# A layer with expert retrieval on one core: 49 gathered pairs moved behind, one dense tile chosen with the queries, half of the later one-hots on VectorE

## The chip, the cores and the metric

One core of one Trainium2 chip. The metric is the device time of one execution in microseconds; a lower one is better. A profiled execution lists its instructions from the first to the last (the span); its own time lies a little above that.

## The reference, cut to what matters

One layer (attention in two forms, then an expert retrieval, then an RMSNorm) is applied to a sample of 256 tokens and a prompt of 1024. The change touches only the expert retrieval of the prompt:

```python
def one_chunk(xc):                                   # 128 tokens
    qry = einsum('cd,dq->cq', xc, w_query)           # 8 heads, 2 halves of 128
    sc = einsum('chpd,hpnd->chpn', qry, sub_keys)    # 128 scores a half
    s_top, i_top = top_k(sc, 16)
    cand = s_top[half 0] + s_top[half 1]             # 16 x 16
    best_s, pos = top_k(cand, 16)
    idx = i_top[half 0] * 128 + i_top[half 1], at pos
    g = softmax(best_s)
    act = gelu(einsum('chkd,cd->chk', expert_u[idx], xc))
    return einsum('chk,chkd->cd', g * act, expert_v[idx])
```

There are 16384 experts; each token takes 128 slots (8 heads of 16), a row of u and one of v for each, 1024 floats wide.

## The kernel before, in words

The last phase, `phase_mixed`, computes this for the eight prompt tiles of 128 tokens in two ways. Five tiles are **gathered** (`GATHERED`): GpSimd fetches the 128 rows of a slot (u and v, 8 KB each, 1.05 MB in all) by an indirect DMA (L1894) into a ring of eight slots. VectorE takes the dot of the u half with h (L2155), ScalarE the gelu (L1984), VectorE multiplies it by the gate (L2147), ScalarE spreads it on small diagonals (L1991), and TensorE adds up the weighted v halves by 32 matmul records a pair of slots (L2289). A pair is a step; a tile has 65 steps with its last, five tiles have 325. GpSimd may fetch a pair when the pair four before it has been used by TensorE.

Three tiles are **dense** (`DENSE`: tiles 5, 6 and 7, 384 tokens together). All experts are computed for them: stage 1 (L2309) multiplies u, turned, by the 384 tokens, ScalarE takes the gelu (L2015), VectorE multiplies by a full matrix of gates (`mult`, L2180), stage 2 (L2325) multiplies by v, and VectorE adds the products up (L2190). This goes in 32 chunks of four key columns, each with 2 MB of u, 2 MB of v and 0.75 MB of gates loaded by SP's queue. The gates matrix is built before, in 96 **blocks** of four tokens (32 a tile): VectorE makes one-hot rows of the first index, times the gate (L2139), ScalarE one-hot rows of the second index by |iota - j| and relu(1 - x) (L1964, L1966), TensorE multiplies them (L2274), ScalarE copies the product out (L1973), and after every eight blocks it issues a store of 2 MB to `gates_d` (L1977) from one of two buffers. A block may begin when the block two before it has been multiplied. Ahead of each dense tile's blocks TensorE turns its indices and gates (`turn`, L2263) and ScalarE copies them (L1950).

Both ways need the choice of the experts. Queries (L2239) and scores (L2253) of all tiles are computed first, 32 queries of 16 matmul records, and the scores go to memory. SP loads them head by head into `SCL` buffers (L1775). A **pick** of a head is the two top-16 lists, the candidates and their top 16 (`choose`, L2049 to L2076); after four heads come the **decode** (L2083 to L2106) and the softmax of the gates.

One list sets the order of all this on every engine: `Turns.walk`. Each engine walks the same list and carries out its own part, in order. `advance(k)` puts k steps there, together with the picks of the gathered tiles that fall due by their step number (`octet`, L1544, L1545). The walk has three parts: the queries (L1574 to L1596), where steps begin with v = 13; the blocks (`turned` and the loops, L1614 to L1625); and the dense part (L1641 to L1655), where the steps left are spread evenly over the units of stage 1 and stage 2 by their cost (L1650):

```python
self.advance(before + round(rest * min(1.0, spent / whole)) - self.e, False)
```

## Time and profile before

| | us |
|---|---|
| median of 3 runs | 4753.62 (4751.6 to 4756.91) |
| the profiled execution, its own time | 4752.96 |
| its span | 4751.2 |
| TensorE busy | 4023.7 (85%) |
| VectorE busy | 2817.4 (59%) |
| ScalarE busy | 1179.1 (25%) |
| GpSimd busy | 1241.0 (26%) |
| read and written in memory | 1366 MB, 288 GB/s over the span |

The shares are means over phases with different limits; the phase that changes begins near 2095 us. A busy TensorE counts matmuls whose ends are modelled. In the rows PE is TensorE, PEld its loading of weights, DVE VectorE, ACT ScalarE, POOL GpSimd, SP the sync engine's queue; L12 is line 12 of the kernel, and an arrow `<-` stands before what is read or waited for. A DMA share is the mean busy share of the core's 16 DMA engines.

### The profile page before, as it was taken

How to read it: one execution, taken by the hardware profiler on the slowest of the kernel's cores; microseconds unless marked ns; L12 is line 12 of the kernel's file. 1: busy time of each engine (PE TensorE's matmuls, PEld its weight loads, DVE VectorE, ACT ScalarE, POOL GpSimd, SP SyncE). 2: the span in 40 equal slices, each digit the busy share in tenths (PEclk: the TensorE clock that was granted, in tenths of full speed). 3: DMA queues.
4: the chain of work that ended last, by engine and by line, in shares of the span. 5: the costliest groups of instructions: out<-in, count | busy, mean ns of one | idle time of the engine just before them, and what ended most of it. 6: DMA issues, size and time to landing. Idle time of an engine off the chain costs nothing.

```text
span 4751.2 us, 61482 instructions
## 1 busy us (share of the span) xinstructions
PE 4023.7 (85%) x22629; PEld 2075.0 (44%) x22629; DVE 2817.4 (59%) x7082; ACT 1179.1 (25%) x3076; POOL 1241.0 (26%) x1018
## 2 busy tenths in 40 slices
PE   7786699996999989979864444589999999999998
PEld 3444444443777754434321222334444444444443
DVE  1323865775888867634668888735454554545434
ACT  0221111221555531121213544711111111111111
POOL 0201322222344223301332233322222222222221
PEclk9888799998999999989875767799999999999999
DMA  6143498986444377646898988999998999889996
GB/s 239 66 173 120 165 360 301 372 334 234 158 165 185 136 305 297 263 182 254 340 356 320 364 336 348 367 341 344 364 362 323 363 359 362 336 335 346 355 359 249
DMA packets 351291, 1370.43 MB, mean 288 GB/s; under 512 B 26896, under 2 KB 112528, under 8 KB 231568
## 3 DMA queue, kind: packets, MB, share of 16 engines
q0 software_dynamic: 129024, 939.58, 50.8%
q1 hardware_dynamic: 161840, 389.17, 22.4%
q10 hardware_dynamic: 60128, 37.75, 2.5%
q8 instruction: 180, 2.95, 0.2%
q14 instruction: 119, 0.97, 0.1%
HBM read 1277.22 MB, written 89.18 MB: 288 GB/s over the span
## 4 chain that ended last, share of the span: by engine, by line
PE 34%; DVE 11%; DMA 7%; issue 3%; ACT 2%; POOL 0%; SPq 0%; DVEq 0%; ACTq 0%; POOLq 0%
PE prompt_exp_wk L2309 13%; PE prompt_exp_wk L2325 11%; PE prompt_exp_acc L2289 6%; DVE prompt_exp_junk L2155 4%; DMA prompt_exp_ring<-in_experts_dram,prompt_exp_idx 3%; PE prompt_exp_wk L2239 3%; DMA gates_dram<-prompt_exp_area 2%; ACT prompt_exp_diag L1991 1%; DVE prompt_exp_topi L2052 1%; DVE prompt_exp_hit L2101 1%; DVE prompt_exp_hT L2139 1%; DVE prompt_exp_top L2049 1%; DMA scores_dram<-prompt_exp_area 1%; DVE prompt_exp_rest L2057 0%; POOL prompt_exp_ring L1894 0%
## 5 line engine op out<-in xcount | busy, mean ns | idle before, releaser
L1894 POOL DMA_INDIRECT prompt_exp_ring<-in_experts_dram,prompt_exp_idx x640 | 686.8, 1073 | 1977.6 <-PE prompt_exp_acc L2289 1758.0
L2155 DVE CUSTOM_DVE_ANT_0 prompt_exp_junk<-prompt_exp_ring,prompt_exp_h 128x1024 bf16<-128x1024 f32 x640 | 761.2, 1221 | 112.2 <-DMA prompt_exp_ring<-in_experts_dram,prompt_exp_idx 112.1
L2309 PE MATMUL prompt_exp_wk<-prompt_exp_hT,prompt_exp_area 128*128 128x384 f32 x2048 | 692.1, 492 | 16.2 <-DMA prompt_exp_area<-in_u_turned_dram 16.2
L2325 PE MATMUL prompt_exp_wk<-prompt_exp_area 128*128 128x512 f32 x1536 | 698.2, 603 | 0.0
L2289 PE MATMUL prompt_exp_acc<-prompt_exp_ring,prompt_exp_diag 32*32 32x512 f32 x10240 | 414.4, 677 | 225.2 <-ACT prompt_exp_diag L1991 224.0
L2190 DVE TENSOR_TENSOR prompt_exp_area<-prompt_exp_area,prompt_exp_wk 128x512 f32<-128x512 f32 x186 | 127.6, 686 | 776.9 <-PE prompt_exp_wk L2325 755.6
L537 PE MATMUL prompt_proj_acc<-normed_w,normed_hT 128*128 128x512 f32 x1280 | 553.8, 595 | 14.4 <-PEq L91 14.4
L2309 PEld LDWEIGHTS prompt_exp_wk<-prompt_exp_hT,prompt_exp_area 128*128 128x128 f32 x2048 | 385.0, 191 | 343.5 <-issue 88.4
L152 POOL DMA_INDIRECT sample_hid_ring<-in_experts_dram,sample_hid_idx x256 | 275.1, 1075 | 898.3 <-DVE sample_hid_acc L182 849.3
L2325 PEld LDWEIGHTS prompt_exp_wk<-prompt_exp_area 128*128 128x128 f32 x1536 | 283.8, 191 | 409.5 <-issue 378.3
L1984 ACT ACTIVATE prompt_exp_ge<-prompt_exp_dot 128x2 f32<-128x2 f32 x320 | 64.8, 203 | 1301.9 <-DVE prompt_exp_dot L2155 1301.4
L537 PEld LDWEIGHTS prompt_proj_acc<-normed_w,normed_hT 128*128 128x128 f32 x1280 | 243.6, 191 | 318.5 <-issue 318.3
L165 DVE CUSTOM_DVE_ANT_0 sample_hid_junk<-sample_hid_ring,sample_hid_h 128x1024 bf16<-128x1024 f32 x256 | 353.9, 1382 | 37.5 <-DMA sample_hid_ring<-in_experts_dram,sample_hid_idx 27.5
L182 DVE SCALAR_TENSOR_TENSOR sample_hid_acc<-sample_hid_ring,sample_hid_w,sample_hid_acc 128x1024 f32<-128x1024 f32 x254 | 330.5, 1301 | 7.4
L2274 PE MATMUL prompt_exp_wk<-prompt_exp_area,prompt_exp_hT 128*128 128x128 f32 x768 | 148.9, 362 | 186.1 <-DVE prompt_exp_hT L2139 137.1
L2289 PEld LDWEIGHTS prompt_exp_acc<-prompt_exp_ring,prompt_exp_diag 32*32 32x32 f32 x10240 | 81.3, 108 | 442.9 <-ACT prompt_exp_diag L1991 350.0
L2274 PEld LDWEIGHTS prompt_exp_wk<-prompt_exp_area,prompt_exp_hT 128*128 128x128 f32 x768 | 132.9, 265 | 249.1 <-DVE prompt_exp_hT L2139 185.3
L2015 ACT ACTIVATE prompt_exp_area<-prompt_exp_wk 128x384 f32<-128x384 f32 x128 | 62.7, 490 | 436.2 <-PE prompt_exp_wk L2309 436.0
L1991 ACT ACTIVATE prompt_exp_diag<-prompt_exp_fold,prompt_exp_wgt 128x32 f32<-128x32 f32 x640 | 165.9, 306 | 16.3 <-DVE prompt_exp_wgt L2147 16.3
L537 PE MATMUL sample_proj_acc<-sample_proj_w,sample_proj_hT 128*128 128x512 f32 x320 | 139.5, 598 | 9.4 <-PEq L271 9.4
L998 PE MATMUL prompt_att_Op<-prompt_att_vB,prompt_att_pT_b 128*128 128x128 f32 x1024 | 125.9, 276 | 10.4 <-ACT prompt_att_pT_a L712 10.4
L1964 ACT ACTIVATE prompt_exp_area<-prompt_exp_iota,prompt_exp_ijgT 128x128 f32<-128x128 f32 x384 | 121.9, 389 | 21.2 <-issue 16.6
(350 smaller groups left out, 5001.5 us busy)
## 6 DMA issues: line engine op xcount, KB each, us to landing
prompt_exp_area<-in_u_turned_dram SPq DMA_DIRECT2D x128, 512.0 KB
prompt_exp_area<-in_experts_dram SPq DMA_DIRECT2D x64, 1024.0 KB
gates_dram<-prompt_exp_area ACTq DMA_DIRECT2D x12, 2048.0 KB, 25.0
prompt_exp_area<-gates_dram SPq DMA_DIRECT2D x32, 768.0 KB, 10.7
sample_proj_w<-in_w_all_dram SPq DMA_DIRECT2D x10, 2048.0 KB, 20.0
normed_w<-in_w_all_dram SPq DMA_DIRECT2D x10, 2048.0 KB, 18.6
proj_dram<-prompt_proj_stage SPq DMA_DIRECT2D x80, 256.0 KB
prompt_exp_ring<-in_experts_dram,prompt_exp_idx POOLq DMA_INDIRECT x640
```

What stands on the lines that cost most here:

```text
L152: self.nc.gpsimd.indirect_dma_start(out=self.ring[:, s % self.RING, :], out_offset=None, in_=self.experts, in_offset=bass.IndirectOffsetOn ...
L165: self.nc.vector.tensor_tensor_reduce(out=self.junk[:], in0=self.ring[:, s % self.RING, 0:D], in1=self.h[:], scale=1.0, scalar=0.0, op0=AL ...
L182: nc.vector.scalar_tensor_tensor(self.acc[:], v, w, self.acc[:], ALU.mult, ALU.add).then_inc(self.added, 1)
L537: last = nc.tensor.matmul(acc[:, u % 4, :], hT[:, k, t * P:(t + 1) * P], w[:, c % NL, k, :], start=(k == 0), stop=(k == KD - 1))
L1894: nc.gpsimd.indirect_dma_start(out=ring[:, s % RING, :], out_offset=None, in_=experts, in_offset=bass.IndirectOffsetOnAxis(ap=idx[:, n % 2 ...
L1991: last = nc.scalar.activation(diag[:, (g - 1) % 2, c, :], fold[:], ACT.Copy, scale=wgt[:, s:s + 1])
L2155: nc.vector.tensor_tensor_reduce(out=junk[:, s % 2, :], in0=ring[:, s % RING, 0:D], in1=h2[:, n % 2, :], scale=1.0, scalar=0.0, op0=ALU.mu ...
L2239: last = nc.tensor.matmul(wk[:, v % 2, :], wq[:, h // 2 % 2, k, at:at + P], (hT1 if grp else hT0)[:, k, :], start=(k == 0), stop=(k == KD ...
L2274: last = nc.tensor.matmul(wk[:, 2 + i % 2, c * KEYS:(c + 1) * KEYS], onehot_a[:, i % 2 * BLOCK + c, :], onehot_b[:, i % 2, c, :], start=Tr ...
L2289: last = nc.tensor.matmul(acc[at:at + Q, part, :], diag[k, (g - 1) % 2, c, :], ring[k, s % RING, D + half * 512:D + half * 512 + 512], sta ...
L2309: last = nc.tensor.matmul(wk[:, j % 2, 0:TURNED], ut[:, j % 3, k, :], hT_dense[:, k, :], start=(k == 0), stop=(k == KD - 1))
L2325: last = nc.tensor.matmul(wk[:, 2 + o % 2, :], act_e[:, c % 2, j, t * P:(t + 1) * P], vt[:, half, j, :], start=(j == 0), stop=(j == JB - 1))
```

## The change

It changes the order and three resources, not what is computed.

- In the query part two steps a query become one and two by turns, and the second dense tile (6) is picked there, beside tile 5. Tile 7's picks stand in the first tile's blocks.
- The first tile's blocks have one step for every two of them, the second tile's one for every four, the third's three for every eight.
- Since two dense tiles are chosen before the first turn, tile 6 has its own buffers: `mid`, `mid_ij`, `mid_gd` in a free piece of `area`, and a third kind in `topi` and `pos`. `SCL` goes from 4 to 3.
- From block 32 on, the second one-hot rows of every odd block are made by VectorE, in one instruction of 128x512 (`is_equal` of iota and the index, both broadcast), and not by ScalarE's five.

The diff, with some context and unchanged parts left out:

```diff
--- before.py
+++ after.py
@@ -1592,8 +1592,10 @@
                 on("gates", GATHERED[0], slice(ends[h], h + 1))
             if 0 <= h < HEADS and at == 2:
                 self.pick_dense(first, h)
+            if h >= 0 and at == 3 and h < HEADS:
+                self.pick_dense(first + 1, h)
             if v >= 13:
-                self.advance(2)
+                self.advance(1 + v % 2)
         done = 0
 
         def blocks(k):
@@ -1611,18 +1613,19 @@
             on("turn", d)
             self.advance(1)
 
-        for d in range(2):
+        turned(0)
+        for k in range(HEADS):
+            self.pick_dense(first + 2, k)
+            for _ in range(2):
+                blocks(2)
+                self.advance(1)
+        for d in (1, 2):
             turned(d)
-            for k in range(HEADS):
-                self.pick_dense(first + d + 1, k)
+            for k in range(BLOCKS // 4):
                 blocks(2)
-                self.advance(2 if k % 2 else 1)
+                self.advance(k % 2 if d == 1 else 1)
                 blocks(2)
-                self.advance(2)
-        turned(2)
-        for k in range(BLOCKS // 2):
-            blocks(2)
-            self.advance(1)
+                self.advance(1 - k % 2)
         on("spread_b", done - 1)
         on("built")
         assert done == len(DENSE) * BLOCKS
@@ -1667,7 +1670,7 @@
 
     with ExitStack() as ctx:
         m = Mem(nc, ctx, [], tag)
-        RING, SCL = 8, 4
+        RING, SCL = 8, 3
         BACK = RING // PAIR
         NQ = P // Q
         NG, ND = len(GATHERED), len(DENSE)
@@ -1677,25 +1680,28 @@
         junk = m.sb("junk", [P, 2, D], mybir.dt.bfloat16)
         ysq, yo = m.sb("ysq", [P, 2, D]), m.sb("yo", [P, D])
         hT0, area = m.sb("hT0", [P, KD, 512]), m.sb("area", [P, 16384])
-        top, topi = m.sb("top", [P, 2, TOPK]), m.sb("topi", [P, 2, 2, 4, TOPK], U32)
+        top, topi = m.sb("top", [P, 2, TOPK]), m.sb("topi", [P, 3, 2, 4, TOPK], U32)
         topb, table = m.sb("topb", [P, 2, 4, TOPK], BF16), m.sb("table", [P, 2, TOPK], BF16)
         rest = m.sb("rest", [P, 2, KEYS])
         cand, crest = rest[:, 0, 0:CANDS], rest[:, 1, 0:CANDS]
         best, soft, ssum = m.sb("best", [P, 3, HEADS, TOPK]), m.sb("soft", [P, 3, HEADS, TOPK]), m.sb("ssum", [P, HEADS])
-        pos, posf = m.sb("pos", [P, 2, 2, 4, TOPK], U32), m.sb("posf", [P, 2, 4, TOPK])
+        pos, posf = m.sb("pos", [P, 3, 2, 4, TOPK], U32), m.sb("posf", [P, 2, 4, TOPK])
         part, ab = m.sb("part", [P, 2, 4, TOPK]), m.sb("ab", [P, 2, 4, TOPK], BF16)
         hit = m.sb("hit", [P, 4, TOPK, TOPK], BF16)
         idx, g2 = m.sb("idx", [P, 2, SLOTS], I32), m.sb("g2", [P, 2, SLOTS])
         dot, ge, wgt = (m.sb(n, [P, SLOTS]) for n in ("dot", "ge", "wgt"))
         diag = m.sb("diag", [P, 2, PAIR, Q])
         scl = m.sb("scl", [P, SCL, 2 * KEYS])
-        ij, gd, ijgT = m.sb("ij", [P, 2, SLOTS]), m.sb("gd", [P, SLOTS]), m.sb("ijgT", [P, 2, 3, P])
+        ij_sb, gd_sb, ijgT = m.sb("ij", [P, 2, SLOTS]), m.sb("gd", [P, SLOTS]), m.sb("ijgT", [P, 2, 3, P])
...
+        mid = area[:, 15360:15616].rearrange("p (a h k) -> p a h k", a=2, h=HEADS)
+        mid_ij, mid_gd = area[:, 15616:15872].rearrange("p (a s) -> p a s", a=2), area[:, 15872:16000]
+        ij, gd = ij_sb[:], gd_sb[:]
         scs = area[:, 14336:15360].rearrange("p (x c) -> p x c", x=2)
...
@@ -1749,6 +1755,27 @@
...
+        def vector_b(i):
+            return i >= BLOCKS and i % 2 == 1
+
+        def scalar_bs(count):
+            return sum(not vector_b(i) for i in range(count))
+
+        def kind_of(tile):
+            return 0 if tile in GATHERED else 1 + (tile - DENSE[0]) % 2
+
+        def best_of(tile):
+            return mid[:, 0] if kind_of(tile) == 2 else best[:, place(tile)]
+
+        def soft_of(tile):
+            return mid[:, 1] if kind_of(tile) == 2 else soft[:, place(tile)]
+
+        def ij_of(d):
+            return mid_ij if d % 2 else ij
+
+        def gd_of(d):
+            return mid_gd if d % 2 else gd
 
         def normed(k):
             return hs_[:, k, :] if k else h2[:, 0, :]
@@ -1939,7 +1966,7 @@
                     nonlocal softened
                     softened += 1
                     act.wait_ge(best_ready, softened)
-                    part = soft[:, place(tile), hs, :]
+                    part = soft_of(tile)[:, hs, :]
                     nc.scalar.activation(part, part, ACT.Exp).then_inc(exp_ready, 1)
 
                 def turn(d):
@@ -1957,8 +1984,10 @@
...
+                    if vector_b(i):
+                        return
                     if i:
-                        act.wait_ge(b_ready, i)
+                        act.wait_ge(b_ready, scalar_bs(i))
...
@@ -2060,7 +2089,7 @@
 
                 def choose(tile, h, part):
                     nonlocal picked
-                    o, c, kind = place(tile), h % 4, int(tile in DENSE)
+                    c, kind = h % 4, kind_of(tile)
                     if part == 0:
                         dve.wait_ge(scl_ld[picked % SCL], 16 * (picked // SCL + 1))
                         top16([(top[:, p, :], topi[:, kind, p, c, :], scl[:, picked % SCL, p * KEYS:(p + 1) * KEYS], rest[:, p, :])
@@ -2075,10 +2104,10 @@
...
@@ -2091,9 +2120,9 @@
                     link(nc.vector.scalar_tensor_tensor(ab[:, 1, c, :], row, 9.0, part[:, 1, c, :], ALU.is_lt, ALU.mult))
                     cols = slice(hs.start * TOPK, hs.stop * TOPK)
                     if tile in DENSE:
-                        if tile > DENSE[0] and hs.start == 0:
-                            dve.wait_ge(ij_turned, tile - DENSE[0])
-                        to = ij[:, :, cols]
+                        if tile == DENSE[2] and hs.start == 0:
+                            dve.wait_ge(ij_turned, 1)
+                        to = ij_of(tile - DENSE[0])[:, :, cols]
                     else:
                         to = part[:, :, c, :].rearrange("p a h k -> p a (h k)")
                     found = hit[:, 0:n, :, :]
@@ -2107,20 +2136,18 @@
                         dve.sem_inc(heads_chosen[tile], n)
 
                 def soften(tile, hs):
-                    o = place(tile)
-                    nc.vector.tensor_tensor(soft[:, o, hs, :], best[:, o, hs, :],
-                                            best[:, o, hs, 0:1].to_broadcast([P, hs.stop - hs.start, TOPK]),
+                    nc.vector.tensor_tensor(soft_of(tile)[:, hs, :], best_of(tile)[:, hs, :],
+                                            best_of(tile)[:, hs, 0:1].to_broadcast([P, hs.stop - hs.start, TOPK]),
                                             ALU.subtract).then_inc(best_ready, 1)
 
                 def gates(tile, hs):
                     nonlocal gated
                     gated += 1
-                    o = place(tile)
-                    to = gd[:] if tile in DENSE else g2[:, tile % 2, :]
+                    to = gd_of(tile - DENSE[0]) if tile in DENSE else g2[:, tile % 2, :]
                     dve.wait_ge(exp_ready, gated)
-                    link(nc.vector.reduce_sum(ssum[:, hs], soft[:, o, hs, :], AXX))
+                    link(nc.vector.reduce_sum(ssum[:, hs], soft_of(tile)[:, hs, :], AXX))
                     link(nc.vector.reciprocal(ssum[:, hs], ssum[:, hs]))
-                    link(nc.vector.tensor_tensor(to.rearrange("p (h c) -> p h c", c=TOPK)[:, hs, :], soft[:, o, hs, :],
+                    link(nc.vector.tensor_tensor(to.rearrange("p (h c) -> p h c", c=TOPK)[:, hs, :], soft_of(tile)[:, hs, :],
                                                  ssum[:, hs].unsqueeze(2).to_broadcast([P, hs.stop - hs.start, TOPK]), ALU.mult))
 
                 def turn(d):
@@ -2134,6 +2161,10 @@
                         dve.wait_ge(q_full, 32)
                     if i >= 2:
                         dve.wait_ge(gp_full, i - 1)
+                    if vector_b(i):
+                        wide = [P, BLOCK, KEYS]
+                        nc.vector.tensor_tensor(onehot_b[:, i % 2, :, :], iota[:].unsqueeze(1).to_broadcast(wide),
+                                                ijgT[:, d % 2, 1, BLOCK * k:BLOCK * k + BLOCK].unsqueeze(2).to_broadcast(wide), ALU.is_equal)
                     for c in range(BLOCK):
                         t = BLOCK * k + c
                         last = nc.vector.tensor_scalar(onehot_a[:, i % 2 * BLOCK + c, :], iota[:], ijgT[:, d % 2, 0, t:t + 1],
@@ -2259,13 +2290,13 @@
                     pe.wait_ge(q_ready, 32)
                     if d:
                         pe.wait_ge(ij_spread, d)
-                    for a, x in enumerate((ij[:, 0, :], ij[:, 1, :], gd[:])):
+                    for a, x in enumerate((ij_of(d)[:, 0, :], ij_of(d)[:, 1, :], gd_of(d))):
                         last = nc.tensor.transpose(wk[:, 0, a * P:(a + 1) * P], x, ident[:])
                     last.then_inc(ij_turned, 1)
 
                 def block_(i):
                     pe.wait_ge(a_ready, i + 1)
-                    pe.wait_ge(b_ready, i + 1)
+                    pe.wait_ge(b_ready, scalar_bs(i + 1))
                     if i < 2:
                         pe.wait_ge(s_ready, 32)
                     else:
```

## Rows read from the trace of the kernel before

**Rows 1.** The page: busy tenths of TensorE and the DMA engines in 40 slices.

```profile
PE   7786699996999989979864444589999999999998
...
DMA  6143498986444377646898988999998999889996
```

**Rows 2.** Stretches, busy us (x instructions) of PE, PEld, DVE, ACT, POOL; clock; DMA share; GB/s.

```profile
2210.00:2450.00 240.00, 201.59 (x1616) 86.18 (x1584) 152.63 (x482) 47.48 (x151) 76.98 (x73) 0.90 0.90 348
2450.00:2551.00 101.00, 34.07 (x499) 8.32 (x499) 80.12 (x281) 16.31 (x54) 30.75 (x31) 0.52 0.89 358
2551.00:2762.00 211.00, 100.31 (x1203) 55.93 (x1203) 182.40 (x646) 102.94 (x291) 63.61 (x60) 0.67 0.87 331
2762.00:2971.00 209.00, 95.88 (x1221) 55.08 (x1219) 181.08 (x628) 98.64 (x290) 62.96 (x59) 0.70 0.91 350
2971.00:3093.00 122.00, 69.42 (x816) 43.63 (x816) 91.70 (x285) 88.71 (x249) 42.41 (x36) 0.79 0.98 367
3093.00:3143.00 50.00, 33.75 (x186) 17.67 (x183) 16.64 (x50) 8.26 (x21) 5.79 (x5) 0.83 0.82 297
3143.00:4733.00 1590.00, 1548.99 (x9547) 697.31 (x9546) 755.25 (x1746) 199.65 (x715) 396.83 (x372) 0.99 0.92 347
```

**Rows 3.** ScalarE's copies of the turned tiles, L1950.

```profile
L1950 ACT COPY prompt_exp_ijgT<-prompt_exp_wk x3: 478/478/478, 2550.8 to 2970.9; 128x384 f32<-128x384 f32 x3
```

**Rows 4.** Stage-1 matmuls of the dense part, L2309.

```profile
L2309 PE MATMUL prompt_exp_wk<-prompt_exp_hT,prompt_exp_area x2048: 486/486/1009, 3093.1 to 4699.5; 128*128 128x384 f32 x187
```

**Rows 5.** Order in time on ScalarE, 2999 to 3013 us.

```profile
2999.74 7.96 ACTq L1977 DMA_DIRECT2D gates_dram<-prompt_exp_area  x1
...
3012.34 0.58 ACT L1973 COPY prompt_exp_area<-prompt_exp_wk 128x512 f32<-128x512 f32 x1 [2.60 <-DMA gates_dram<-prompt_exp_area]
```

**Rows 6.** Gates stores, L1977: issue on ScalarE's queue, time to landing.

```profile
L1977 ACTq DMA_DIRECT2D gates_dram<-prompt_exp_area x12: 366/370/8425, 2606.9 to 3091.7; - x12
...
DMA to landing us min/median/max: 19.0/25.0/34.2
```

**Rows 7.** TensorE's groups in 3143 to 4720: busy us, mean ns, idle before.

```profile
L2289 PE MATMUL prompt_exp_acc<-prompt_exp_ring,prompt_exp_diag 32*32 32x512 f32 x5984 | 216.6, 607 | 36.4 <-ACT prompt_exp_diag L1991 35.2 <-DVE prompt_exp_ysq L2166 1.3
```

**Rows 8.** Order in time on VectorE, 2975 to 3012 us.

```profile
2977.13 0.48 DVE L2049 MAX8 prompt_exp_top<-prompt_exp_scl 128x8 f32<-128x128 f32 x2
...
2981.98 2.14 DVE L2139 TENSOR_SCALAR prompt_exp_hT<-prompt_exp_iota,prompt_exp_ijgT 128x128 f32<-128x128 f32 x8
2984.03 0.15 DVE L2147 TENSOR_TENSOR prompt_exp_wgt<-prompt_exp_ge,prompt_exp_g 128x2 f32<-128x2 f32 x1
...
2986.39 2.14 DVE L2139 TENSOR_SCALAR prompt_exp_hT<-prompt_exp_iota,prompt_exp_ijgT 128x128 f32<-128x128 f32 x8
...
3002.45 0.22 DVE L2083 CAST prompt_exp_topb<-prompt_exp_topi 128x128 bf16<-128x128 uint32 x1
...
3009.30 1.22 DVE L2104 TENSOR_REDUCE prompt_exp_part<-prompt_exp_hit 128x64 f32<-128x1024 bf16 x1
```

**Rows 9.** VectorE's groups in 2551 to 2971: busy us, mean ns, idle before.

```profile
L2155 DVE CUSTOM_DVE_ANT_0 prompt_exp_junk<-prompt_exp_ring,prompt_exp_h 128x1024 bf16<-128x1024 f32 x117 | 139.7, 1220 | 23.9 <-DMA prompt_exp_ring<-in_experts_dram,prompt_exp_idx 23.9
...
L2101 DVE TENSOR_TENSOR prompt_exp_hit<-prompt_exp_ab,prompt_exp_table 128x1024 bf16<-128x1024 bf16 x12 | 14.7, 1225 | 0.4
...
L2147 DVE TENSOR_TENSOR prompt_exp_wgt<-prompt_exp_ge,prompt_exp_g 128x2 f32<-128x2 f32 x59 | 9.2, 156 | 17.7 <-ACT prompt_exp_ge L1984 16.0 <-issue 1.0
```

**Rows 10.** DMA in 3143 to 4720: in all, and the gathers' queue.

```profile
DMA packets 111819, 551.25 MB, mean 350 GB/s; under 512 B 9744, under 2 KB 11664, under 8 KB 64016
...
q0 software_dynamic: 53665, 390.76, 64.0%
```

**Rows 11.** DMA in 2675 to 2725: busy tenths of 40 slices, and in all.

```profile
DMA  9999999999999999999999999999999999999999
...
DMA packets 7063, 20.08 MB, mean 402 GB/s; under 512 B 351, under 2 KB 4821, under 8 KB 5015
```

**Rows 12.** Waits in 2225 to 2450: us in total, times, longest.

```profile
DVE prompt_exp_junk L2155 <- DMA prompt_exp_ring<-in_experts_dram,prompt_exp_idx: 66.8, 38, 3.1
```

More of the change, by code:

```diff
@@ L2077, in choose @@
                                                  top[:, 1, 0:1].to_broadcast([P, TOPK - HALF_ROWS]), ALU.add))
-                    top16([(best[:, o, h, :], pos[:, kind, 0, c, :], cand, crest)])
+                    top16([(best_of(tile)[:, h, :], pos[:, kind, 0, c, :], cand, crest)])
                 def decode(tile, hs):
-                    n, kind = hs.stop - hs.start, int(tile in DENSE)
+                    n, kind = hs.stop - hs.start, kind_of(tile)
                     c, square = slice(hs.start % 4, hs.start % 4 + n), [P, n, TOPK, TOPK]
```

## The prediction

> **What bounds the kernel now.** I read the page first: over the last third TensorE stands at nine tenths, and the DMA engines stand at eight or nine tenths in nearly all of the second half [rows 1]. So there are two candidates, TensorE and the DMA engines, and an average cannot choose between them. The table by stretches does [rows 2]. I cut it at the three turns (where ScalarE copies a turned tile: 2550.8, 2762 and 2970.9 us, the first and the last of three in [rows 3]) and at the first stage-1 matmul (3093.1 us [rows 4]). Five stretches matter:
>
> - 2210 to 2450, queries with gathered steps beside them: TensorE 201.6 of 240 us, DMA share 0.90.
> - 2450 to 2551, the end of the query part: VectorE 80 of 101 us, TensorE 34.
> - 2551 to 2762 and 2762 to 2971, the blocks of the first two dense tiles: VectorE 182.4 of 211 and 181.1 of 209 us. VectorE sets these.
> - 2971 to 3093, the blocks of the third tile: VectorE 92, ScalarE 89 of 122 us, but DMA share 0.98. Here the DMA engines set the pace: the issue of a gates store took 7.96 us [rows 5] where the median is 0.37 [rows 6], and a copy behind it waited 2.60 us for a store to land [rows 5].
> - 3093 to the end, the dense part: in 3143 to 4733 TensorE is busy 1549 of 1590 us at a granted clock of 0.99, so at the 2.4 GHz level. Its step matmuls waited for ScalarE's diagonals 35.2 us in all [rows 7]. TensorE sets this part. But the DMA engines are at 0.92 beside it, 347 GB/s. They are the next bound, and a close one.
>
> **The change by its parts.** Counting the walk (the list of calls is the same for all engines): the steps issued at the three turns and at the end of the blocks were 53, 83, 113, 130 and become 40, 58, 68, 81, of 325. So 49 steps, 98 row gathers of 1.05 MB, 102.8 MB, go from the part ahead into the dense part.
>
> *Prices.* From the order in time on VectorE [rows 8]: a step is 2.36 us where it waits for nothing (2984.03 to 2986.39), a pick 4.85 (2977.13 to 2981.98), a decode of four heads 8 (from 3002.45; its last big reduction starts at 3009.30). In the first two tiles' blocks the dots waited 23.9 us and the weights 17.7 over 59 steps, 0.7 a step [rows 9]; so a step removed gives between 2.4 and 3.1, and I take 3.0, since these waits are the steps' own. A step on TensorE: 216.6 us busy for 187 steps (5984 records at 32 a step) = 1.16 us [rows 7]. A one-hot by one VectorE instruction of 128x512, both inputs broadcast: not in the trace. The nearest is the comparison of 128x1024 bf16 elements with broadcast inputs at 1225 ns [rows 9]: half of it, 0.61, for 512 elements. The ends are 0.5 (a float row may start cheaper) and 1.23 (a float element may cost two of bf16); I use 0.7, near the half. There are 32 of them, 22 us, between 16 and 39.
>
> *Query part, to the first turn* (before 2551). 13 steps leave; tile 6's eight picks and two decodes come in and tile 1's four picks go: on VectorE -39 + 19 + 16 = -4 us. Up to the last query VectorE has room (152.6 of 240 us [rows 2]), so there TensorE's side counts: 9 steps x 1.16 = -10. Behind the last query, where VectorE sets the pace, 13 steps instead of 17, five picks instead of seven, one decode more: -12 - 10 + 8 = -14. Together -24; the ends are 0 (the picks moved ahead delay the dots, and the queries with them) and -35.
>
> *First tile's blocks.* 12 steps fewer (30 to 18), one pick more (13 for 12): -36 + 5 = -31; 211 becomes 180. Ends -20 and -40.
>
> *Second tile's blocks.* 30 steps become 10, 11 picks one, three decodes none, 16 one-hots come: 209 - 60 - 10 x 4.85 - 24 + 11 = 87 us on VectorE. ScalarE's 98.6 us [rows 2] are for 32 blocks and 30 steps; with half of its one-hots and 20 steps gone it has some 55. What is late next is the gates store: four of 2 MB in this stretch, two buffers, so a stretch of eight blocks cannot be shorter than one store's landing, 25 us median, 19 to 34 [rows 6]. Four of them are 76 to 136. I take 95, near the VectorE sum and the median: -114, ends -75 and -124.
>
> *Third tile's blocks.* 17 steps become 13. The stretch is DMA-limited, and 8 gathers at 2.7 us of all 16 engines (0.640 x 1577 us for 390.76 MB [rows 10]) are 22 us; the store's latency stays: -17, ends 0 and -30.
>
> *Queues moved past.* With three score buffers for four, SP issues each score load one pick nearer to its use, and in order: it waits there for a buffer, with the loads of h and x behind it. Tile 6's eight loads now stand between the query part's. A pick that comes before its load holds every dot behind it on VectorE. The largest wait of a dot for a row was 3.1 us [rows 12]; I take +5 for the whole, from 0 to +15. POOL's order of gathers is the same, and a tile's decodes stay at the same step numbers, so it waits for no list longer than before. The third kind of buffers (topi, pos, mid) adds no instruction, only room; tile 7's decode still waits for the first turn, long past.
>
> Ahead of the dense part: -24 - 31 - 114 - 17 + 5 = **-181 us**; the blocks end near 2912.
>
> *Dense part.* Before it takes 3093 to 4751, 1658 us. For TensorE 49 steps at 1.16 add 57. VectorE takes 49 steps, six picks and two decodes more (45 picks stood ahead before, 39 do now): 118 + 29 + 16 = 163 us on 755 of 1590 [rows 2], hidden beside TensorE and the transfers. For the DMA engines, 566 MB (551 in 3143 to 4720 [rows 10] and 297 GB/s in the 50 us before [rows 2]) become 671 MB with 102.8 for the gathers and some 2 for scores and one more tile's h, x and output. At what rate? The engines' own figure is 347 at a share of 0.92 [rows 2], 377 at a full one. But the rate goes up where more is queued: 402 GB/s over 2675 to 2725, with small gates stores among the gathers, where the share was full [rows 11]. When the DMA engines are the bound, gathers and weights are queued always. I take 386, between 377 and 402 and nearer to the row of the same mix: 671 / 386 = 1738. To that come the tail without transfers, 4720 to 4751, 31 us; the thin start, 50 x (1 - 297/386) = 12; and some 10 for the closing of tiles. Sum 1791: **+133**, ends +57 (TensorE) and +209 (370 GB/s).
>
> The sum: 4752.96 (the profiled execution; its span of 4751.2 and 1.8 around it) - 181 + 133 = **4705**. The median of the runs, 4753.62, is 0.7 above the profiled one; nothing is corrected for it.
>
> **The rivals.**
>
> *TensorE stays the bound of the dense part*: then +57, 4753 - 181 + 57 = 4629. For it: TensorE waits for so little now, and rates above 400 exist [rows 11]. Against: 671 MB in 1640 + 57 us is 395 GB/s as a mean over the whole part, its thin start and every closing of a tile included. 0.14.
>
> *The DMA engines saturate at what they show per full share*: slower than before. The break-even rate follows from 1658 + 181 - 53 = 1786 us for 671 MB: 376 GB/s. Its place is the ring of eight rows: where steps come as densely as they will, in the queries, dots waited 66.8 us for rows in 225 us [rows 12]; TensorE was busy only 201.6 of 240 us there, and its granted clock was 0.90, between the levels of 1.2 and 2.4 GHz, so a part of that time ran at the lower [rows 2]. At 370 GB/s the dense part is 671 / 370 + 53 = 1867, +209, and the time 4781. For: 377 is what the dense rows give at full share, and 358 GB/s, share 0.89, is the rate of 2450 to 2551 [rows 2]. 0.25.
>
> *The rate does not rise at all with what is queued*: the 350 GB/s of the dense part [rows 10] is then a ceiling, 671 / 350 + 53 = 1970, +312, 4884. Against it stand 20 MB at 402 [rows 11]; these could be the exception. 0.03. Beside it stands a rule of the Trainium skill, "DMA: Bandwidth & Descriptors", section "Where 436 GB/s comes from": for transfers between HBM and SBUF the HBM side binds, at about 358 GB/s. By that figure the dense part would be an estimated 671 / 358 + 53 = 1927 us, and the kernel 4841. By that rule the trace agrees in the mean of the dense part and disagrees in the 50 us at 402.
>
> *The blocks do not get shorter as they should*: the gates stores and the picks moved ahead hold them, and only -110 of the -181 comes. Then 4753 - 110 + 133 = 4776, or about no change with a better dense rate. For: landings of 34.2 us exist [rows 6]. Against: gathers, which such a store shares the engines with, become a third as many there. 0.10.
>
> **How the numbers follow.** The forecast has 0.48, from 396 to 378 GB/s 4661 to 4742. A measurement here can tell about 0.2%, 9.5 us. Faster: 0.44 of the forecast, 0.14 of the first rival, 0.02 of the last: 0.60. Within 0.2%: 0.04 of the forecast, 0.06 of the second, 0.03 of the last: 0.13. Slower: 0.19, 0.03 and 0.05: 0.27. The range takes in the first rival's 4629 and the second's to some 366 GB/s, and with that the last rival: 4625 to 4800. What is left out is the ceiling at 350 and the tails.
>
> **What would show it.** Turns nearer to each other: first at about 2527, then +180, +95, and the first stage-1 matmul near 2912. VectorE's new group, 32 instructions near 0.7 us; ScalarE's Abs down from 384 to 256. In the dense part: DMA share 0.97 or more at 380 to 392 GB/s, VectorE waiting for rows, TensorE below 97% busy and a part of its time waiting for diagonals. I am wrong if the dense rate is under 376 (slower) or TensorE is as busy as before (much faster), or if the blocks end after 2950.

## The result and the profile after

The changed kernel takes 4601.75 us (median of 4 runs, 4596.18 to 4608.61), the kernel before 4752.61 beside it: a ratio of 0.9684, interval 0.9667 to 0.9701. It is 151 us faster, where 48 us had been forecast, and outside the range.

The kernel after was cut into stretches at its own three turns (2497.6, 2664.0 and 2759.7 us), its last query (2407.6) and its first stage-1 matmul (2855.8). The columns are those of [rows 2]: bounds, length, busy us (x instructions) of PE, PEld, DVE, ACT and POOL, granted clock, DMA share, GB/s.

```profile
2210.00:2407.60 197.60, 178.19 (x1264) 80.19 (x1263) 150.65 (x543) 41.94 (x123) 55.74 (x52) 0.94 0.84 319
2407.60:2497.60 90.00, 30.28 (x453) 8.85 (x451) 72.84 (x243) 15.69 (x47) 24.87 (x25) 0.56 0.81 315
2497.60:2664.00 166.40, 83.84 (x835) 56.25 (x835) 158.40 (x619) 91.41 (x253) 37.73 (x38) 0.66 0.76 279
2664.00:2759.70 95.70, 52.00 (x563) 37.59 (x563) 73.00 (x225) 59.16 (x148) 16.26 (x17) 0.84 0.83 297
2759.70:2855.80 96.10, 56.86 (x672) 40.39 (x673) 79.09 (x236) 55.25 (x153) 28.42 (x28) 0.84 0.99 365
2855.80:4599.50 1743.70, 1653.68 (x11362) 724.90 (x11361) 953.70 (x2251) 257.10 (x904) 528.09 (x475) 0.98 0.97 387
```

The same cuts in the kernel before, which the text reads below. [Rows 2] had its first two cuts at round times, so the queries' end (2442.4) differs a little:

```profile
2210.00:2442.40 232.40, 196.91 (x1535) 83.43 (x1504) 145.80 (x450) 45.31 (x145) 75.05 (x70) 0.90 0.90 351
2442.40:2550.80 108.40, 38.76 (x581) 11.07 (x579) 86.78 (x310) 18.29 (x59) 32.49 (x33) 0.56 0.89 353
3093.10:4751.20 1658.10, 1587.37 (x9780) 715.70 (x9776) 782.72 (x1808) 216.50 (x749) 402.63 (x376) 0.98 0.91 343
```

Part by part, in us:

| part | before | after | difference | forecast |
|---|---|---|---|---|
| queries and their end, to the first turn | 340.8 | 287.6 | -53.2 | -24 and +5 |
| first tile's blocks | 211.6 | 166.4 | -45.2 | -31 |
| second tile's blocks | 208.5 | 95.7 | -112.8 | -114 |
| third tile's blocks | 122.2 | 96.1 | -26.1 | -17 |
| ahead of the dense part | 883.1 | 645.8 | -237.3 | -181 |
| dense part | 1658.1 | 1743.7 | +85.6 | +133 |
| sum | | | -151.7 | -48 |

Two terms are off: what the steps were worth ahead of the dense part, and what they cost in it. (One of the 49 steps is the closing of a tile, which gathers nothing. So 48 pairs moved, 96 gathers and 100.7 MB, where the title and the prediction have 49, 98 and 102.8.) The new VectorE instruction is not one of them. Its group in the kernel after:

```profile
L2166 DVE TENSOR_TENSOR prompt_exp_area<-prompt_exp_iota,prompt_exp_ijgT x32: 676/688/699, 2666.6 to 2852.3; 128x512 f32<-128x512 f32 x32
```

The prediction assumed 0.7 us for it, and it takes 0.688. Now the dense part after. First the DMA engines in 2906 to 4568 (in all, and the gathers' queue), as in [rows 10]:

```profile
DMA packets 126802, 653.49 MB, mean 393 GB/s; under 512 B 11408, under 2 KB 14224, under 8 KB 66774
...
q0 software_dynamic: 67392, 490.76, 72.9%
```

then TensorE's steps in it, as in [rows 7] (busy us, mean ns, idle before):

```profile
L2320 PE MATMUL prompt_exp_acc<-prompt_exp_ring,prompt_exp_diag 32*32 32x512 f32 x7520 | 270.9, 604 | 44.4 <-ACT prompt_exp_diag L2020 43.4 <-DVE prompt_exp_ysq L2197 0.9
```

The rate rose from 350 to 393 GB/s, as the forecast had said it would under a longer queue. But TensorE's waits for diagonals rose only from 35.2 to 43.4 us, and TensorE is still busy 1653.7 of 1743.7 us. Both bounds are close here, and a profile with both near full does not say which of them ends last. That took runs.

### The profile page after: what moved, and what is told of

The parts are those of the page before. It is cut to its first block, busy times and chain, and to the rows that moved or that the text cites. A ratio compares the mean times of both kernels' runs of the same rounds, so it can differ in the third digit from the quotient of the medians.

```text
span 4599.5 us, 61350 instructions
## 1 busy us (share of the span) xinstructions
PE 3988.8 (87%) x22629; PEld 2057.9 (45%) x22629; DVE 2836.5 (62%) x7114; ACT 1128.4 (25%) x2916; POOL 1254.2 (27%) x1018
## 4 chain that ended last, share of the span: by engine, by line
PE 34%; DVE 10%; DMA 6%; issue 3%; ACT 2%; POOL 0%; SPq 0%; DVEq 0%; ACTq 0%; another core or an unknown queue 0%
PE prompt_exp_wk L2340 13%; PE prompt_exp_wk L2356 11%; PE prompt_exp_acc L2320 6%; DVE prompt_exp_junk L2186 4%; PE prompt_exp_wk L2270 4%; DMA prompt_exp_ring<-in_experts_dram,prompt_exp_idx 3%; DMA gates_dram<-prompt_exp_area 2%; DVE prompt_exp_hT L2170 1%; DVE prompt_exp_hit L2130 1%; DVE prompt_exp_topi L2081 1%; ACT prompt_exp_diag L2020 1%; PE prompt_exp_wk L2305 1%; DVE prompt_exp_top L2078 0%; DMA scores_dram<-prompt_exp_area 0%; PE prompt_exp_wk L2284 0%
## 5 line engine op out<-in xcount | busy, mean ns | idle before, releaser
L1921 POOL DMA_INDIRECT prompt_exp_ring<-in_experts_dram,prompt_exp_idx x640 | 698.6, 1092 | 1815.9 <-PE prompt_exp_acc L2320 1603.4
L2340 PE MATMUL prompt_exp_wk<-prompt_exp_hT,prompt_exp_area 128*128 128x384 f32 x2048 | 697.5, 495 | 23.7 <-DMA prompt_exp_area<-in_u_turned_dram 23.7
L2320 PE MATMUL prompt_exp_acc<-prompt_exp_ring,prompt_exp_diag 32*32 32x512 f32 x10240 | 392.9, 643 | 173.5 <-ACT prompt_exp_diag L2020 170.3
L2305 PE MATMUL prompt_exp_wk<-prompt_exp_area,prompt_exp_hT 128*128 128x128 f32 x768 | 132.7, 342 | 112.9 <-DVE prompt_exp_hT L2170 76.4
L2305 PEld LDWEIGHTS prompt_exp_wk<-prompt_exp_area,prompt_exp_hT 128*128 128x128 f32 x768 | 122.3, 250 | 157.8 <-DVE prompt_exp_hT L2170 102.3
L174 DVE TENSOR_TENSOR sample_hid_w<-sample_hid_ge,sample_hid_g 128x1 f32<-128x1 f32 (+1 forms) x208 | 59.1, 284 | 115.0 <-ACT sample_hid_ge L203 114.8
```

Source lines behind the costliest of these rows:

```text
L1921: nc.gpsimd.indirect_dma_start(out=ring[:, s % RING, :], out_offset=None, in_=experts, in_offset=bass.IndirectOffsetOnAxis(ap=idx[:, n % 2 ...
L2305: last = nc.tensor.matmul(wk[:, 2 + i % 2, c * KEYS:(c + 1) * KEYS], onehot_a[:, i % 2 * BLOCK + c, :], onehot_b[:, i % 2, c, :], start=Tr ...
L2320: last = nc.tensor.matmul(acc[at:at + Q, part, :], diag[k, (g - 1) % 2, c, :], ring[k, s % RING, D + half * 512:D + half * 512 + 512], sta ...
L2340: last = nc.tensor.matmul(wk[:, j % 2, 0:TURNED], ut[:, j % 3, k, :], hT_dense[:, k, :], start=(k == 0), stop=(k == KD - 1))
```

## The experiments

**Which part of the change gives the gain.** The change has three parts: 49 steps moved (S), tile 6 chosen with the queries (T), VectorE's one-hot rows (V). Four kernels took them apart.

The changed kernel without V:

```diff
         def vector_b(i):
-            return i >= BLOCKS and i % 2 == 1
+            return False
```

> The changed kernel with all second one-hot rows made by ScalarE again (VectorE's 32 instructions of 0.69 us gone, ScalarE's five back). Theory G (the gates stores and the DMA engines set the second and third tile's blocks, 96 us each): both stretches stay within 5 us, time 4602 to 4612. Theory E (the engines' own work sets them): ScalarE goes from 59 to about 88 us and from 55 to 84 of 96 us in them and waits more for TensorE between, so each gets 8 to 20 us longer, time 4618 to 4642.

4602.93 us, ratio 0.9684 (0.9668 to 0.9700), the same as with V. The second and third tile's blocks of this kernel:

```profile
2657.30:2757.00 99.70, 66.80 (x563) 48.01 (x563) 64.35 (x209) 86.58 (x229) 17.31 (x17) 0.72 0.81 284
2757.00:2857.20 100.20, 65.74 (x673) 44.27 (x673) 70.73 (x221) 82.38 (x234) 31.12 (x28) 0.75 0.99 359
```

ScalarE is at 87 and 82 of 100 us and not at 59 and 55 of 96. The stretches get 4 us longer each. In the whole time that does not show: the first turn of this profile comes 6.6 us earlier (2491.0 for 2497.6), in a part that V does not touch. Theory G's numbers came, both stretches within 5 us and the time in its range. So ScalarE's own work does not set these stretches; what holds them near 96 to 100 is not isolated here.

The kernel before with S alone:

```diff
-                self.advance(2)
+                self.advance(1 + v % 2)
...
-        for d in range(2):
+        for d in range(3):
             turned(d)
             for k in range(HEADS):
-                self.pick_dense(first + d + 1, k)
+                if d < 2:
+                    self.pick_dense(first + d + 1, k)
                 blocks(2)
-                self.advance(2 if k % 2 else 1)
+                self.advance(k % 2 if d == 1 else 1)
                 blocks(2)
-                self.advance(2)
+                self.advance(1 if d == 0 else 1 - k % 2)
-        turned(2)
-        for k in range(BLOCKS // 2):
-            blocks(2)
-            self.advance(1)
```

> The kernel before with only the steps moved: 40, 58, 68, 81 at the turns and the end of the blocks, tile 6 still picked in the first tile's blocks, ScalarE making all second rows, four score buffers. Theory of the prediction's sums (queries set by TensorE, a step 1.16 us there and 3.0 where VectorE sets the pace): queries -22, blocks -36, -60, -17, dense part +86: 4753 - 49 = about 4704. Theory R (in the queries the steps waited for their rows, so each step there is worth 3.5 to 5 us): queries -50, the rest the same: about 4675.

4622.40 us, ratio 0.9727 (0.9711 to 0.9744): 131 of the 151 us, and more than either theory gave. Its stretches up to the third turn:

```profile
2210.00:2388.30 178.30, 168.62 (x1209) 76.18 (x1208) 119.79 (x399) 39.26 (x116) 54.40 (x50) 0.97 0.89 344
2388.30:2468.40 80.10, 30.68 (x453) 9.85 (x451) 56.63 (x175) 15.80 (x46) 26.21 (x25) 0.57 0.89 358
2468.40:2635.60 167.20, 82.62 (x836) 56.57 (x835) 158.22 (x619) 91.34 (x253) 37.25 (x38) 0.68 0.76 278
2635.60:2770.40 134.80, 69.74 (x563) 50.51 (x563) 114.21 (x453) 87.50 (x228) 15.44 (x17) 0.69 0.63 219
```

The queries lost 54.1 us for 9 steps and their end 28.3 us for 4 steps and four picks, which fall due later with the steps. The 54.1 is a little too large. All these stretches are cut at 2210 us, but the query part does not begin at the same time in every profile. Taken from the first step's matmuls on TensorE (2209.7 us before, 2205.4 here) to the last query, the stretch went from 232.7 to 182.9 us. That is 49.8 us for 9 steps, 5.5 us for one, at much the same rate of the DMA engines (350 and 339 GB/s). The two row gathers of a step are 5.4 us of all 16 DMA engines, the price in the prediction; TensorE's 1.16 us is a fifth of the 5.5. The end lost about what the prediction's prices give, 4 x 3.0 + 4 x 4.85 = 31.

The blocks lost 44.4, 73.7 and 23.2 us, where both theories had 36, 60 and 17, and the queries with their end 82.4, where they had 22 and 50. The dense part of this kernel is 1744.3 us, as in the changed one and as both theories had it.

The kernel before with T alone (the step counts of before, ScalarE's rows):

```diff
+            if h >= 0 and at == 3 and h < HEADS:
+                self.pick_dense(first + 1, h)
...
-        for d in range(2):
+        turned(0)
+        for k in range(HEADS):
+            self.pick_dense(first + 2, k)
+            blocks(2)
+            self.advance(2 if k % 2 else 1)
+            blocks(2)
+            self.advance(2)
+        for d in (1, 2):
             turned(d)
             for k in range(HEADS):
-                self.pick_dense(first + d + 1, k)
                 blocks(2)
-                self.advance(2 if k % 2 else 1)
+                self.advance(1 if d == 2 or k % 2 == 0 else 2)
                 blocks(2)
-                self.advance(2)
+                self.advance(2 if d == 1 else 1)
```

> The kernel before with only tile 6 picked in the queries and tile 7 in the first tile's blocks (with its buffers, three score buffers), steps 53, 83, 113, 130 as before, no VectorE rows. By the prediction's sums VectorE has room of 87 us in the first 240 us of the queries, but 47 to 65 us of picks and decodes come in: the second tile's blocks lose 40 us of picks and 16 of decodes if nothing else sets them, the queries gain 0 to 30: time 4725 to 4750. Theory R (rows set the queries): what comes in is hidden in waits, and the second tile's blocks, with 30 steps and stores, become DMA-limited at about 170: 4715 to 4735. If the picks hold the dots back: 4753 or more.

4744.59 us, ratio 0.9981 (0.9971 to 0.9992), a gain of some 9 us and in the range of the first theory. Its second tile's blocks:

```profile
2775.40:2955.00 179.60, 95.76 (x1219) 52.64 (x1219) 131.55 (x384) 97.90 (x290) 64.78 (x59) 0.74 1.00 393
```

VectorE has 49 us less to do in them, but the stretch becomes 28.9 us shorter and no more: the DMA share is 1.00. In this stretch Theory R had the mechanism, with 170 us for 179.6. The picks that came into the queries and their end cost 14.4 us there. So T pays more where the steps are gone: beside S the second tile's blocks go from 134.8 (S alone) to 99.7 (S and T), and the time from 4622.4 to 4602.9.

The kernel before with V alone (the edits of the diff to `vector_b`, `scalar_bs` and `build_a`, without the others):

```diff
+                    if vector_b(i):
+                        wide = [P, BLOCK, KEYS]
+                        nc.vector.tensor_tensor(onehot_b[:, i % 2, :, :], iota[:].unsqueeze(1).to_broadcast(wide), ...)
```

> The kernel before with only VectorE making the second rows of every odd block from block 32. VectorE sets the second tile's blocks (181 of 209 us), so +11 us there; the third tile's are DMA-limited (share 0.98), 0. Time 4760 to 4768. If ScalarE's five instructions were on the chain there (a rival), the third stretch gets 10 us or more shorter and the time is 4745 to 4755.

4756.51 us, ratio 1.0006 (0.9996 to 1.0016): no difference that can be measured, and a time between the two expected ranges. In the profile the second tile's blocks took 214.0 us for 208.5 and the third's 120.9 for 122.2. That is the first theory's order with half of its cost. The profiled execution took 4771.04 us; most of what it lies above the median came in its queries, 11.9 us longer than before, which V does not touch.

**What sets the queries.** The kernel before with half of each query's matmuls; it leaves out half of the sum over d in the queries, and so picks other experts:

```diff
-                    for k in range(KD):
+                    for k in range(KD // 2):
...
-                                                start=(k == 0), stop=(k == KD - 1))
+                                                start=(k == 0), stop=(k == KD // 2 - 1))
```

> The kernel before with four of the eight matmuls of every query: it leaves out half of the sum over d, TensorE does some 110 us less in the queries, the transfers stay; the picks find other experts, so other rows are gathered, as many. Theory of the prediction (TensorE sets the queries up to the last one, 232 us from 2210): that stretch gets 50 to 60 us shorter for its 18 queries beside steps. Theory R (the steps wait for their rows there, at a DMA share of 0.90): from query 13 on it gets less than 25 us shorter; the time falls by what the first 13 queries give, 15 to 45 us, and little more.

4724.47 us, ratio 0.9934 (0.9917 to 0.9951). The queries with steps beside them, from the first step's matmuls to the last query, first before and then in this kernel:

```profile
2209.70:2442.40 232.70, 197.21 (x1536) 83.66 (x1536) 146.06 (x453) 45.31 (x145) 75.05 (x70) 0.90 0.90 350
2186.20:2420.20 234.00, 144.69 (x1392) 56.99 (x1393) 147.80 (x468) 45.69 (x147) 74.58 (x70) 0.77 0.87 342
```

TensorE is busy 53 us less here, and the stretch is no shorter. The 22 us by which the last query comes earlier were all gained ahead of the first step, where only queries run. That is Theory R. (One pick waited 17.1 us for its scores here and 4.8 before; with those 12 us taken off, the stretch would still be 222.) Nine steps fewer took 50 us off the same stretch. So it was not TensorE that set it, though it was busy for 85% of it; the steps' way through gather, dot, gelu, diagonal did. How much of the 5.5 us a step is transfer and how much the way back to a free ring slot, no run here separates.

**What sets the dense part.** Two kernels take a load away from one side each. The changed kernel with half of each u from the fourth on, so that stage 1 uses stale halves:

```diff
+                    ks = KD if j < 3 else KD // 2
-                    sp.dma_start(ut[:, j % 3, :, :], u_turned[j]...)
+                    sp.dma_start(ut[:, j % 3, 0:ks, :], u_turned[j]...[:, 0:ks, :])
```

> The changed kernel with only half of each turned u loaded from the fourth on: it leaves out 33 MB of 671 in the dense part and computes stage 1 with stale halves. Theory P: the dense part stays within 15 us of 1744 (the shorter loads may shorten its first stall by a few). Theory D: 33 MB at 393 GB/s are 83 us, dense part 1660 to 1680, time 4520 to 4535.

The changed kernel with four of the eight matmuls of each stage-1 product:

```diff
-                    for k in range(KD):
+                    for k in range(KD // 2):
...
-                                                start=(k == 0), stop=(k == KD - 1))
+                                                start=(k == 0), stop=(k == KD // 2 - 1))
```

> The changed kernel with only four of the eight matmuls of each stage-1 product: it leaves out half of the sum over d, TensorE does some 338 us less, and all transfers stay. The dense part then shows what the DMA engines can do. By the prediction's term they carry 671 MB at 386 GB/s, 1791 us: the dense part would stay at 1740 or more. If they can do 402 to 415 GB/s, and TensorE set the dense part: 671/402 to 671/415 + 50, 1665 to 1720, time 4520 to 4578. A time under 4500 would say that 420 GB/s is no bound.

Without 33 MB the time is 4589.97 us, some 12 less, not the 83 of Theory D. With TensorE relieved it is 4543.40, in the range given for a dense part that TensorE set. The dense part of each, first that of the kernel with half of u, then that of the one with half of stage 1:

```profile
2857.40:4590.90 1733.50, 1651.59 (x11362) 724.41 (x11360) 950.02 (x2249) 256.36 (x904) 530.89 (x474) 0.98 0.95 370
```

```profile
2855.50:4542.20 1686.70, 1385.48 (x10338) 550.36 (x10336) 955.34 (x2249) 249.84 (x904) 534.82 (x474) 0.94 0.99 399
```

So TensorE sets the dense part at 244 steps, and the DMA engines stand at most 57 us behind: they carry it in 1686.7 us, 399 GB/s with the start and the tail in it, at a share of 0.99. The prediction had 1791 for the same. TensorE is not alone, though: 268 us of its work gone gave only these 57.

**Where the DMA engines take over.** Fewer steps ahead, so more in the dense part. One step a query, 68 ahead:

```diff
-                self.advance(1 + v % 2)
+                self.advance(1)
```

> The changed kernel with one step a query, so 27, 45, 55, 68 steps at the turns and the end of the blocks, 13 fewer ahead. Theory P (TensorE still sets the dense part, a step costs there the 1.75 us that 49 steps cost in it): dense part +23; the queries, now at 0.84 DMA share and 178 of 198 us of TensorE, give 13 to 25 back: time 4600, between 4595 and 4612. Theory D (the DMA engines, share 0.97 in the dense part, set it already): 13 steps are 26 gathers at 2.6 us, dense part +68, time 4640 or more.

and with it one step for four blocks in the first tile's blocks, 60 ahead:

```diff
             for _ in range(2):
                 blocks(2)
-                self.advance(1)
+                self.advance(_)
```

> As the run with 68 ahead, and one step for four blocks in the first tile's blocks, so 27, 37, 47, 60. VectorE sets that stretch: 8 steps off it at 2.7 to 4 us give 22 to 32. Theory P: dense part +14 beyond the run with 68, so that time -8 to -18. Theory D: dense part +42 beyond it, so that time +10 to +20.

68 ahead: 4589.04 us (4585.98 to 4590.15), ratio 0.9656 (0.9638 to 0.9675). That is below the 4595 to 4612 of Theory P: the queries and their end became 40.2 us shorter, where 13 to 25 were expected. The first tile's blocks also became 20.6 shorter and the other two 18.1 longer, since picks fall due by the number of steps, and three of them and a decode left the first. 60 ahead: 4625.81, ratio 0.9736 (0.9717 to 0.9755), 37 us more than with 68, where even Theory D had 10 to 20. Its 8 steps gave 15.8 us in the first tile's blocks, not 22 to 32, and cost 62.2 in the dense part, not 42.

The dense part of each, first with 68 ahead, then with 60:

```profile
2813.10:4586.70 1773.60, 1669.33 (x11778) 726.53 (x11777) 995.67 (x2343) 267.09 (x944) 550.22 (x500) 0.98 0.98 395
```

```profile
2786.10:4621.90 1835.80, 1698.34 (x12018) 734.51 (x12016) 1019.09 (x2408) 275.99 (x970) 578.81 (x515) 0.97 0.97 390
```

| steps in the dense part | its time | for each step more | VectorE's dots waited for gathered rows, 2900 to 4560 |
|---|---|---|---|
| 195 | 1658.1 | | |
| 244 | 1743.7 | 1.75 | 116.8 |
| 257 | 1773.6 | 2.3 | 217.8 |
| 265 | 1835.8 | 7.8 | 245.6 |

Behind the first 100 us and up to the last 29, the same two:

```profile
2913.10:4557.70 1644.60, 1573.33 (x11106) 683.69 (x11105) 939.16 (x2229) 244.24 (x879) 525.99 (x477) 0.99 1.00 402
2886.10:4592.90 1706.80, 1612.53 (x11453) 696.43 (x11451) 970.25 (x2306) 250.61 (x907) 559.20 (x496) 0.98 1.00 400
```

At 257 steps the DMA engines have just become full (share 1.00, 402 GB/s), and the price of a step is still near Theory P's. Beyond, it jumps. The last 8 steps are seven pairs and the closing of a tile: 14.7 MB, an estimated 37 of the 62 us at 402 GB/s. The rest is in part a thinner start, in which the closing falls (2849 us): the second 50 us carry 295 GB/s for 413 with 68 ahead, 5.9 MB less, an estimated 15 us. So there is a place where the DMA engines take over, as the prediction said, but it lies 13 to 21 steps beyond 244 and not before it. The waits for rows agree: the kernel with half of stage 1, whose dense part the DMA engines limit, has 233.7 us of them in the same window.

**The stall at the start of the dense part.** After three stage-1 products TensorE stood still for the fourth u, whose load SP issues behind its wait for the last gates store. The kernel after, waits in 2855 to 2950:

```profile
PE prompt_exp_wk L2340 <- DMA prompt_exp_area<-in_u_turned_dram: 23.7, 1, 23.7
```

```diff
                 def stage1(j):
                     if j + 3 < KEYS:
                         load_u(j + 3)
+                    if j == 1:
+                        all_built()
...
-                walk(spread_s=spread_s, choose=choose, step=step, built=all_built, stage1=stage1, ...)
+                walk(spread_s=spread_s, choose=choose, step=step, stage1=stage1, ...)
```

> The changed kernel with SP issuing the loads of the fourth and fifth u before it waits for the gates stores (the loads of gates and v come behind them). In the changed kernel TensorE stood 23.7 us at 2877 to 2901 for the fourth u, since SP waited for the last gates store first. If this stall is on the path of a part that TensorE sets: -15 to -24 us, 4578 to 4587. If the DMA engines set the dense part, the start is only moved: within 8 us of 4602.

4594.16 us, ratio 0.9659 (0.9643 to 0.9676); the interval overlaps that of the changed kernel. The dense part is 1742.9 us, 0.8 shorter. In 2853 to 2950 TensorE's wait for u falls from 23.7 to 4.4 us, but its wait for diagonals rises from 2.5 to 19.3: VectorE now stands 19.8 us before the gates, and the dots stand behind it. The time is in the second expectation's range, but not for its reason, since TensorE sets this dense part. The stall did not go, it moved. With 68 ahead as well:

> Both: one step a query (68 ahead) and the fourth and fifth u before the gates. If the two are independent, the sum of both differences to 4602. If the saved stall only uncovers the DMA engines, it is no better than the run with the u first alone.

4590.52 us, ratio 0.9650 (0.9632 to 0.9668), with a dense part of 1777.5: not the sum of both differences, and no better than 68 ahead alone (4589.04). So this part of the start is not worth an edit in this form.

**The best version.** 68 ahead, and V left out:

> The kernel with 68 steps ahead (one step a query), and ScalarE making all second one-hot rows. With 68 ahead the second and third tile's blocks are 105 us each with VectorE at 86 and 84, so VectorE's 16 instructions of 0.69 us in each may now cost, and ScalarE at 57 to 59 has room for 29 more. Theory G (these stretches are held by the stores and the chain between engines, the rows are nobody's bound): the same as with VectorE's rows, 4584 to 4594. Theory E (VectorE's sum sets them once picks are there): 5 to 15 us faster, under 4584. If ScalarE becomes the bound: over 4594. It also repeats the gain of 68 ahead over 81 in another call, which should stay at 8 to 18 us.

4586.75 us (4584.34 to 4595.49), ratio 0.9653 (0.9640 to 0.9667). V is worth nothing here either: the second and third tile's blocks are 101.2 and 108.5 us for 105.0 and 104.9, and the time is in Theory G's range. By the medians 68 ahead lies 13 and 15 us below the changed kernel. The interval touches that of the changed kernel at 0.9667, so this is a gain of some 0.3% at the edge of what the measurement resolves. Three kernels with 68 ahead took 4586.8 to 4590.5 us and three with 81 took 4594.2 to 4602.9; the nearest two of these, both with the u first, are 3.6 us apart.

## Why the prediction was wrong

*The reading of the bounds* was wrong in two places. For the queries I took TensorE, busy 201.6 of 240 us, and had the rows' waits at hand [rows 12], but used them for a rival alone. For the dense part after I took the DMA engines; TensorE kept it. VectorE in the end of the queries and in the first two tiles' blocks held up, in the main: work taken from it shortened them. The DMA engines as the bound of the third's blocks rest on their share (0.98 before, 0.99 after) and on V giving nothing there; no run takes transfers alone away.

*Query part, -24 and +5: measured -53.2.* The failed step is "there TensorE's side counts: 9 steps x 1.16 = -10". A step there was worth 5.5 us (steps alone: -49.8 for the nine), and half of the queries' matmuls gave nothing beside the steps. The other side was wrong too: "VectorE has room" for tile 6's picks, yet they cost time. From the first step to the last query it is 182.9 us with steps alone, and with the picks 195.7 in the changed kernel and 192.4 in the one without V: 10 to 13 us. The two errors partly cancelled. The end of the queries was priced about right: -14 forecast, -18.4 measured.

*First tile's blocks, -31: measured -45.2.* The term of the sum that was mis-sized is the step at 3.0 us. With the pick that comes in, 12 steps gave about 50 us, 4.2 each. VectorE's busy time fell by 24.6 us; the rest is idle time, 28.6 us before and 8.0 after (211.6 - 182.96 and 166.4 - 158.4). I had spread the waits evenly over all steps; 20.6 of the 28.6 us went with twelve of the thirty.

*Second tile's blocks, -114: measured -112.8,* at 95.7 us for 95. The closeness is in part luck. The sum of VectorE's work had said 87 with nothing else in the way, and VectorE is busy 73. I took 95 for four gates stores one behind the other, but in the trace only one of the four held a copy back, for 7.6 us:

```profile
ACT prompt_exp_area L2002 <- DMA gates_dram<-prompt_exp_area: 7.6, 1, 7.6
```

No run isolates the stores, and what sets the rest of the stretch stays open.

*Third tile's blocks, -17: measured -26.1,* with the DMA share still at 0.99. Four steps, a pick and a decode left it and 16 one-hots came, so no price of a step follows from it alone. One gates store held a copy back here too, for 9.2 us.

*Dense part, +133: measured +85.6.* The failed step is "671 / 386 = 1738" with 53 us of ends on top. The DMA engines can do the part in 1686.7 us (half of stage 1), 104 less than my 1791: behind the first 100 us they run at 408 GB/s there, not 386. The 402 GB/s of [rows 11] with only the tail on top, 671 / 402 + 31 = 1700, would have been near. So the first rival, given 0.14, was the true case: TensorE stays the bound. It had +57; TensorE's busy time rose by 66.3 (1587.4 to 1653.7, 55 of it in the steps' matmuls), its waits for diagonals rose from 35.5 to 45.9 and those for u from 16.2 to 23.7. Against this rival I had set 395 GB/s, from 1640 + 57 us; with my own 1658 it is 391, and the measured mean is 387. The sign that I had named for it, TensorE as busy as before, is the one that came: 0.97 of 2906 to 4568, as in 3143 to 4720 before.

*The rivals.* The ceiling at 350 GB/s is refuted by the dense part at 393 (387 with its ends). The rule of the Trainium skill cited beside it ("DMA: Bandwidth & Descriptors", section "Where 436 GB/s comes from"), some 358 GB/s for transfers with HBM, does not hold for one core alone here: 653 MB went at 393 in 1662 us. The DMA engines at 376 or less: refuted by the same row. "The blocks do not get shorter": refuted. The picks moved ahead did cost time before the first turn, 20 to 23 us with the end of the queries, but the steps taken out there more than paid.

## What to carry to other kernels

A stretch in which an engine is 85% busy and another waits for data may well be set by the latter: take work from each side in turn before pricing a move, and count from an event, not from a round time. Waits are not spread evenly over the items of a stretch: a step taken out gave 4.2 us where VectorE's busy time says 2.4, and 5.5 where TensorE's says 1.2. And a load is moved best from a stretch where its own resource is the bound to one where that resource has room behind another's bound, up to the knee: here 62 steps more were cheap (1.75 to 2.3 us), and the next 8, with a tile's closing among them, cost 7.8 each.

## What the runs showed of the hardware

The DMA engines' rate did not grow in proportion to their busy share. In the dense part before it was 350 GB/s at a share of 0.92, which would make 380 at a full one. With more gathers it was 393 at 0.99 (2906 to 4568) and, with 68 steps ahead, 402 at 1.00. So a share of 0.92 left room for some 15% more, where the share says 9%. The mix changed little and does not explain it, since both queues got faster for the time that they were busy: the gathers' from 387 to 405 GB/s (390.76 MB in 0.640 of 1577 us, 490.76 in 0.729 of 1662), the loads' from 360 to 381 (159.01 MB in 0.280, 161.00 in 0.254). That it is the longer queue that does it is my reading; no run changes the queue alone. Taking the rate at a full share from a part that is not saturated gave too low a ceiling.
